# A two-block network on one core: a first turn split in two, column sums folded through DRAM, and residual rows behind three norms moved to GpSimd

## The chip, the core and the metric

The kernel runs on one core of one Trainium2 chip. The metric is the device time of one execution in microseconds. In what follows PE is TensorE, ACT is ScalarE, DVE is VectorE, POOL is GpSimd, and SP is the queue that starts most of the DMAs.

## The reference, cut to what matters

Two blocks of two layers each run one behind the other on 512 tokens of width 1024. Every layer takes scales, shifts and gates from a projection of a condition vector `c`, and uses them around a mixer (mLSTM, differential attention, RWKV-7, forgetting attention) and a feed-forward part.

```python
cs = jax.nn.silu(c)
for i in range(DEPTH):
    ada = cs @ w_ada[i] + b_ada[i]                       # 6 x 1024 values
    sh1, sc1, g1, sh2, sc2, g2 = jnp.split(ada, 6, axis=-1)
    u = x * (1.0 + sc1) + sh1
    y = mixer(u, ...)                                    # u @ w_in first
    x = _layer_norm(DEEPNORM_ALPHA * x + (1.0 + g1) * y, ln_g[i, 0], ln_b[i, 0])
    u = x * (1.0 + sc2) + sh2
    y = _conv_ffn(u, f_w_up[i], ...)                     # conv, gelu(g) * a, w_down
    x = _layer_norm(DEEPNORM_ALPHA * x + (1.0 + g2) * y, ln_g[i, 1], ln_b[i, 1])
...
mod = c_act @ mod_w[i] + mod_b[i]                        # the second block, the same way
```

## The kernel before, in words

Every product with a weight matrix is a `Linear`, and its work goes in **turns**. A turn gives a group of four PSUM banks; the two groups take turns. A weight tile is 1 MB (128 x 2048 floats; 768 KB in the down projections) and lies in a ring of three slots. SP loads it, ACT rounds it into `w_high` (`act_split`), DVE subtracts that into `w_low` (`dve_split`), and each product is three matmuls (`product`: high by high, high by low, low by high). A turn of a kind "f" linear has two tiles and 96 matmuls of 128 x 512; tiles are split two ahead of their use (`AHEAD`).

The input `u` of a linear comes out of `pe_turn` (transposes of `x_natural`), `act_turn` (scale and shift into `stage`, and the high part for odd k tiles) and `dve_turn` (the low part, and the high part for even k tiles): eight k tiles, 128 x 512 each.

**The projections of `c`.** They are cut into blocks of 512 columns, 4 at the start (`first_ada`, 0 to 3) and 48 spread over the turns of the linears from `m_qk` to `r_out` (`ada_ring`). For each of the 48, DVE multiplies eight 128 x 512 pieces by a column of silu(c) and sums them in `ada_acc` (`dve_ada`, eight instructions at the head of a turn). At the end of the same turn PE sums over the 128 partitions by four matmuls of a 128 x 128 part of `ada_acc` with a column of ones (`pe_ada`), and DVE adds the bias (`dve_ada_take`). The start must have blocks 0 and 2 before the k tiles 0 to 3 of the first `u`, and 1 and 3 before the k tiles 4 to 7.

**The start** is in `pe_first`, `dve_first` and `act_first`, and the order of the loads in `sync_program`: constants, blocks 0 and 2, weight tile 0, blocks 1 and 3, weight tile 1, seventeen small parameter rows, then the turns of `m_qk`.

**Rows behind a norm.** Behind three of the norms, `x_natural` is first used as the unit-variance rows, and its gain and shift are put on later by DVE, two 128 x 1024 instructions a token tile, at the head of the first four turns of `f0_up0`, `d_qk` and `f1_up0` (`dve_ln_rows`). In an `f*_up` turn DVE also runs the convolution of four banks (`f_a`, `f_g`), two `w_low` and the product of the halves.

**Gates** are stored to DRAM as columns (`act_gate_store`) and loaded back as rows on all partitions (`act_gate_load`); the residual on DVE (`dve_residual`) waits for them before it does anything else.

All engines run their programs in the order in which they are written; semaphores tie them together. POOL has nothing to do before the RWKV mixer.

## Time and profile before

| | us |
|---|---|
| median of three runs | 3160.3 |
| lowest, highest | 3153.82, 3168.22 |
| the profiled execution, its own time | 3167.36 |
| its span (first to last instruction) | 3166.0 |
| PE busy | 3006.9 |
| DVE, ACT, POOL busy | 1982.2, 1091.1, 97.6 |
| granted PE clock, mean | 0.982 |

The table is read so: PE is busy for 95% of the span, and the span is 1.4 us under the execution's own time. A saving on PE's own work or in its waits is a saving in the end; a saving on another engine is one only where PE waits for it. In a row of the trace the first number is the start in us, the second the time in us. A product of fp32 that is not split shows as two records. A count behind "x" merges records that follow each other.

### The profile page before, as it was taken

How to read it: one execution, taken by the hardware profiler on the slowest of the kernel's cores; microseconds unless marked ns; L12 is line 12 of the kernel's file. 1: busy time of each engine (PE TensorE's matmuls, PEld its weight loads, DVE VectorE, ACT ScalarE, POOL GpSimd, SP SyncE). 2: the span in 40 equal slices, each digit the busy share in tenths (PEclk: the TensorE clock that was granted, in tenths of full speed). 3: DMA queues.
4: the chain of work that ended last, by engine and by line, in shares of the span. 5: the costliest groups of instructions: out<-in, count | busy, mean ns of one | idle time of the engine just before them, and what ended most of it. 6: DMA issues, size and time to landing. Idle time of an engine off the chain costs nothing.

```text
span 3166.0 us, 46111 instructions
## 1 busy us (share of the span) xinstructions
PE 3006.9 (95%) x19763; PEld 2441.4 (77%) x19788; DVE 1982.2 (63%) x3051; ACT 1091.1 (34%) x1667; POOL 97.6 (3%) x116
## 2 busy tenths in 40 slices
PE   6999999999988999998999999999999998899999
PEld 5877788887866888884877778778887777778887
DVE  5856897787468896787455677654444255554353
ACT  2334432233146432233333333342224344542122
POOL 0000000000000000000002222000000001000000
PEclk8999999999999999998999999999999999999999
DMA  7751554545530454542210000233322220032232
GB/s 230 192 160 54 181 179 163 183 160 173 189 105 21 157 196 146 200 163 65 95 49 11 13 13 10 103 89 104 93 93 95 83 91 27 8 107 93 94 106 80
DMA packets 236545, 346.09 MB, mean 109 GB/s; under 512 B 19621, under 2 KB 121965, under 8 KB 236341
## 3 DMA queue, kind: packets, MB, share of 16 engines
q1 hardware_dynamic: 221236, 329.63, 32.3%
q10 hardware_dynamic: 15104, 13.52, 1.4%
q8 instruction: 155, 2.54, 0.3%
q14 instruction: 50, 0.40, 0.0%
HBM read 340.97 MB, written 2.15 MB: 108 GB/s over the span
## 4 chain that ended last, share of the span: by engine, by line
PE 80%; DVE 11%; ACT 4%; DMA 3%; issue 1%; SPq 0%; DVEq 0%; ACTq 0%
PE bank L141 79%; DVE w_tiles L150 2%; PE bank L144 1%; DVE w_low L150 1%; DMA first_ada<-in_w_ada 1%; ACT w_high L147 1%; DMA weight_ring<-in_d_w_in 1%; DVE ada_acc L162 1%; DVE w_g L150 1%; ACT w_tiles L147 1%; DVE x_natural L162 1%; ACT stage L147 1%; ACT L147 0%; DVE x_sm L168 0%; DVE x_natural L150 0%
## 5 line engine op out<-in xcount | busy, mean ns | idle before, releaser
L150 DVE TENSOR_TENSOR w_low<-weight_ring,w_high 128x2048 fp32r<-128x2048 f32 (+2 forms) x212 | 463.7, 2187 | 455.0 <-ACT w_high L147 454.8
L147 ACT ACTIVATE w_high<-weight_ring 128x2048 fp32r<-128x2048 f32 (+2 forms) x212 | 388.1, 1831 | 610.4 <-DMA weight_ring<-in_mlp_down 179.2
L141 PE MATMUL bank<-u_high,w_high 128*128 128x512 f32 x1472 | 577.3, 392 | 12.0 <-DVE w_low L150 6.2
L141 PE MATMUL bank<-u_high,w_low 128*128 128x512 f32 x1472 | 573.8, 390 | 0.0
L141 PE MATMUL bank<-u_low,w_high 128*128 128x512 f32 x1472 | 573.8, 390 | 0.0
L141 PE MATMUL bank<-w_high,u_high 128*128 128x512 f32 x896 | 353.1, 394 | 7.2 <-DVE w_low L150 2.5
L141 PE MATMUL bank<-w_low,u_high 128*128 128x512 f32 x896 | 350.9, 392 | 0.0
L141 PE MATMUL bank<-w_high,u_low 128*128 128x512 f32 x896 | 350.6, 391 | 0.0
L141 PEld LDWEIGHTS bank<-u_high,w_high 128*128 128x128 f32 x1472 | 276.9, 188 | 70.3 <-ACT stage L147 7.0
L141 PEld LDWEIGHTS bank<-u_high,w_low 128*128 128x128 f32 x1472 | 276.9, 188 | 58.3
L141 PEld LDWEIGHTS bank<-u_low,w_high 128*128 128x128 f32 x1472 | 277.0, 188 | 56.7
L162 DVE SCALAR_TENSOR_TENSOR ada_acc<-ada_ring,silu_c,ada_acc 128x512 f32<-128x512 f32 x336 | 252.6, 752 | 15.6 <-DVE ada_acc L162 0.5
L141 PEld LDWEIGHTS bank<-w_high,u_high 128*128 128x128 f32 x896 | 169.4, 189 | 45.8 <-DVE w_low L150 2.9
L141 PE MATMUL bank<-w_high,g_hidden_low 128*128 128x512 f32 x512 | 199.2, 389 | 0.0
L141 PE MATMUL bank<-w_high,g_hidden_high 128*128 128x512 f32 x512 | 199.2, 389 | 0.0
L141 PE MATMUL bank<-w_low,g_hidden_high 128*128 128x512 f32 x512 | 199.2, 389 | 0.0
L141 PEld LDWEIGHTS bank<-w_high,u_low 128*128 128x128 f32 x896 | 169.5, 189 | 36.0
L141 PEld LDWEIGHTS bank<-w_low,u_high 128*128 128x128 f32 x896 | 169.6, 189 | 34.9
L150 DVE TENSOR_TENSOR g_relu<-g_relu 128x512 f32<-128x512 f32 x64 | 44.3, 692 | 153.8 <-ACT g_relu L147 153.8
L141 PE MATMUL bank<-w_high,f_hidden_high 128*128 128x512 f32 x352 | 138.0, 392 | 1.5 <-DVE w_low L150 1.5
L141 PE MATMUL bank<-w_high,f_hidden_low 128*128 128x512 f32 x352 | 137.1, 389 | 0.0
L141 PE MATMUL bank<-w_low,f_hidden_high 128*128 128x512 f32 x352 | 137.0, 389 | 0.0
(411 smaller groups left out, 4398.9 us busy)
## 6 DMA issues: line engine op xcount, KB each, us to landing
ada_ring<-in_mod_w SPq DMA_DIRECT2D x48, 1024.0 KB, 7.6
weight_ring<-in_f_w_up SPq DMA_DIRECT2D x44, 1024.0 KB, 5.1
ada_ring<-in_w_ada SPq DMA_DIRECT2D x40, 1024.0 KB, 7.3
weight_ring<-in_mlp_up SPq DMA_DIRECT2D x32, 1024.0 KB, 5.5
weight_ring<-in_mlp_down SPq DMA_DIRECT2D x32, 1024.0 KB, 5.0
weight_ring<-in_f_w_down SPq DMA_DIRECT2D x24, 768.0 KB, 4.6
weight_ring<-in_m_w_in SPq DMA_DIRECT2D x16, 1024.0 KB, 10.4
weight_ring<-in_d_w_in SPq DMA_DIRECT2D x12, 1024.0 KB, 5.2
```

What stands on the lines that cost most here:

```text
L141: return self.e.matmul(out, l, r, start=start, stop=stop, skip_group_check=True)
L144: return self.e.transpose(out, in_, ident) if self.live else QUIET
L147: return self.e.activation(out, in_, f, **kw) if self.live else QUIET
L150: return self.e.tensor_tensor(out, a, b, op) if self.live else QUIET
L162: return self.e.scalar_tensor_tensor(out=out, in0=a, scalar=s, in1=b, op0=op0, op1=op1)
```

## The change

1. **The opening.** Weight tile 1 is loaded before blocks 1 and 3. The parameter rows come behind the loads of `m_qk`, and the small gate weights of ACT (`act_m_loads`) behind its whole opening. The splits of tiles 0 and 1 move ahead. The first turn of `m_qk` is done in two sets of k tiles: 0 to 3 for all four banks, then, once blocks 1 and 3 are there, 4 to 7. Block 1 is no longer summed by DVE: ACT scales its eight pieces and POOL adds them up by seven instructions.
2. **Column sums through DRAM.** `ada_acc` is stored to a DRAM scratch (SP, 256 KB), and loaded back so that the four 128-column parts lie side by side with partition and column regrouped. POOL adds four parts to one (128 x 256, then 128 x 128), and PE sums over groups of partitions by one matmul with a 128 x 4 pick matrix. The fold of a block is now due at the end of the turn behind the one in which it was summed. One block moves from `r_out` to `d_out`, and the 12 behind it by one turn. As their gate is ready later, gate `f0` is stored, awaited and loaded by ACT at the end of `f0_up0`.
3. **Residual rows.** The gain and shift behind the three norms go from DVE to POOL.

```diff
-                Linear("d_out", "t", a["d_w_out"][0], 2, wide(0), ada=blocks("m0", 11, 1))]
-        lin += [Linear("f1_up0", "f", up[1], 6, halves(0), ada=blocks("m1", 0, 6)),
+                Linear("d_out", "t", a["d_w_out"][0], 2, wide(0), ada=blocks("m0", 11, 1) + blocks("m1", 0, 1))]
+        lin += [Linear("f1_up0", "f", up[1], 6, halves(0), ada=blocks("m1", 1, 6)),
                 Linear("f1_dn0", "t", down[1], 2, wide(0), 12, 0, ada=blocks("kv", 0, 2)),
-                Linear("f1_up1", "f", up[1], 5, halves(6), ada=blocks("m1", 6, 5)),
...
             turn += x.turns
-            for i, b in enumerate(x.ada or ()):
-                self.ada_bank[b] = x.group(i)
+            for i, b in enumerate(x.ada):
+                if summed is not None:
+                    self.takes[x.name, i] = summed
+                summed = b
+        self.takes["r_r", 0] = summed
...
         self.sp_weight(sp, 0)
+        self.sp_weight(sp, 1)
         for b in (1, 3):
             self.sp_first(sp, b)
-        self.sp_weight(sp, 1)
+        self.sp_linear(sp, "m_qk")
         for name, dst, src, last in self.param_parts():
             if dst[0] > 0:
                 sp.dma_start(self.rows[dst[1]:dst[2], dst[0], :], src).then_inc(*self.params_in.landed(*(("rows",) if last else ())))
-        self.sp_linear(sp, "m_qk")
+        sp.wait_ge(self.G, "first summed", 1)
...
                 if w >= AHEAD:
                     self.sp_weight(sp, w)
+                if name != "d_out" or w > L.first + i * per:
+                    self.sp_sum_in(sp)
             if i < len(L.ada):
...
                 sp.wait_ge(self.V, "ada used", b - 1, s)
+                if s:
+                    self.sp_sum_out(sp, b - 1)
             src = w[s * 512:(s + 1) * 512, :].rearrange("(k p) n -> p k n", p=P)
             dst = self.aring[:, s, :].rearrange("p (k n) -> p k n", k=4)
             sp.dma_start(dst, src).then_inc(*self.ada_in[s].landed(b))
+
+    def sp_sum_out(self, sp, b):
+        sp.wait_ge(self.V, "ada summed", b)
+        if b - 2 >= len(self.ada_first):
+            sp.wait_ge(self.fold_in, b - 2)
+        sp.dma_start(self.fold_rows[b % 2], self.aacc[:]).then_inc(*self.fold_out.landed(b))
+        self.stored_sum = b
+
+    def sp_sum_in(self, sp):
+        b = self.stored_sum
+        if b > self.loaded_sum:
+            tile, passed = self.sum_place(b)
+            sp.wait_ge(self.fold_out, b)
+            if passed:
+                sp.wait_ge(*passed)
+            if b > len(self.ada_first):
+                sp.wait_ge(self.T, "ada", b - 1)
+            src = self.fold_rows[b % 2].rearrange("a n -> (a n)").rearrange("(q p m) -> p q m", q=4, p=P)
+            sp.dma_start(tile.rearrange("p (q m) -> p q m", q=4), src).then_inc(*self.fold_in.landed(b))
+            self.loaded_sum = b
+
+    def sum_place(self, b):
...
+    def pool_sums(self, g, *names, rows=None):
+        for name in names:
+            for i in range(self.lin[name].turns):
+                if rows and i < TT:
+                    self.pool_ln_rows(g, *rows[:3], i, rows[3])
+                if (name, i) in self.takes:
+                    b = self.takes[name, i]
+                    parts = self.sum_place(b)[0].rearrange("p (q m) -> p q m", q=4)
+                    g.wait_ge(self.fold_in, b)
+                    g.tensor_tensor(parts[:, 0:2, :], parts[:, 0:2, :], parts[:, 2:4, :], ALU.add).then_inc(*self.G.up())
+                    g.wait_ge(self.G)
+                    g.tensor_tensor(parts[:, 0, :], parts[:, 0, :], parts[:, 1, :], ALU.add).then_inc(*self.G.up("folded", b))
...
                 between()
 
-    def pe_ada(self, pe, b):
-        bank = self.ada_bank.get(b, 7)
-        pe.wait_ge(self.V, "ada summed", b)
-        if bank in self.free:
-            pe.wait_ge(*self.free[bank])
-        for j in range(4):
-            m = pe.matmul(self.bank[bank][:, j:j + 1], self.aacc[:, j * P:(j + 1) * P], self.ones[:, 0:1], True, True)
-        m.then_inc(*self.T.up("ada", b))
-        self.free[bank] = (self.V, "mod", b)
-
-    def dve_ada_take(self, v, b):
-        _, bias, at, _ = self.ada_blocks[b]
-        v.wait_ge(self.T, "ada", b)
-        v.tensor_tensor(self.mod[:, at:at + 4], self.bank[self.ada_bank.get(b, 7)][:, 0:4], bias, ALU.add).then_inc(
-            *self.V.up("mod", b))
+    def pe_ada(self, pe, name, i):
+        if (name, i) in self.takes:
+            b, bank = self.takes[name, i], self.lin[name].group(i)
+            pe.wait_ge(self.G, "folded", b)
...
-                    v.wait_ge(self.V)
                     if b > len(self.ada_first):
-                        v.wait_ge(self.T, "ada", b - 1)
+                        v.wait_ge(self.fold_out, b - 1)
                     v.tensor_scalar(self.aacc[:], src, col, None, ALU.mult).then_inc(*self.V.up())
...
-    def dve_ln_rows(self, v, st, tiles, n, t, turned):
+    def pool_ln_rows(self, g, st, tiles, n, t, turned):
         x = self.X[:, t, :]
-        v.wait_ge(self.T, "turned", turned, KT - 1)
-        v.wait_ge(self.ln_in[n], "rows")
-        v.wait_ge(self.V)
-        v.tensor_tensor(x, x, tiles[0][:], ALU.mult).then_inc(*self.V.up())
-        v.wait_ge(self.V)
-        v.tensor_tensor(x, x, tiles[1][:], ALU.add).then_inc(*self.V.up("rows", st, t))
+        g.wait_ge(self.T, "turned", turned, KT - 1)
+        g.wait_ge(self.ln_in[n], "rows")
+        g.tensor_tensor(x, x, tiles[0][:], ALU.mult).then_inc(*self.G.up())
+        g.wait_ge(self.G)
+        g.tensor_tensor(x, x, tiles[1][:], ALU.add).then_inc(*self.G.up("rows", st, t))
...
         scale, shift = self.plain_modulation(0)
         for h in range(2):
+            if h == 0:
+                self.act_split(a, 0)
             a.wait_ge(self.V, "first", h)
             a.wait_ge(self.V, "first", 2 + h)
-            if h:
-                self.act_split(a, 0)
             self.act_turn(a, "m u", scale, shift, range(4 * h, 4 * h + 4))
-        self.act_split(a, 1)
+            if h == 0:
+                self.act_split(a, 1)
+                for k in range(KT):
+                    src = self.first_w[:, 1, k, :]
+                    a.wait_ge(self.first_in[1][k // 4], "first")
+                    a.activation(src, src, ACT.Copy, scale=self.cs[:, k:k + 1]).then_inc(*self.A.up("first scaled", k))
...
-        self.pe_turn(pe, "m u", lambda t: self.X[:, t, :])
-        for b, bank in ((1, 3), (3, 2)):
+        x = lambda t: self.X[:, t, :]
+        self.pe_turn(pe, "m u", x, range(6))
+        self.pe_first_turn(pe, range(4))
+        for b, bank in ((1, 6), (3, 7)):
             pe.wait_ge(*self.free[bank])
             self.pe_first_summed(pe, b, bank)
             self.free[bank] = (self.V, "first", b)
+        self.pe_turn(pe, "m u", x, range(6, KT))
+        self.pe_first_turn(pe, range(4, KT))
+        self.pe_ada(pe, "m_qk", 0)
+
+    def pe_first_turn(self, pe, kts):
+        L = self.lin["m_qk"]
+        for s in range(2):
+            w = L.tile(0, s)
...
+            for kt in kts:
+                for n in range(2):
+                    b = 2 * s + n
+                    bank, o = L.group(0) + b, kt * 256 + n * P
+                    if kt == 0 and bank in self.free:
+                        pe.wait_ge(*self.free[bank])
+                    pe.wait_ge(self.V, "u", "m u", kt)
+                    m = self.product(pe, self.bank[bank][:], [y[:, w % SLOTS, o:o + P] for y in (self.whigh, self.wlow)],
+                                     [y[:, kt, :] for y in self.u], kt == 0, kt == KT - 1)
+                    if kt == KT - 1:
+                        m.then_inc(*self.T.up("sum", "m_qk", 0, b))
+                        self.free[bank] = (self.V, "got", "m_qk", 0, b)
+            if kts[-1] == KT - 1:
+                self.T.mark("used", w)
...
         self.dve_first_sums(v, 2)
         self.dve_first_take(v, 0, 6)
         self.dve_first_take(v, 2, 7)
+        self.dve_split(v, 0)
         self.dve_turn(v, "m u", range(4))
-        self.dve_first_sums(v, 1)
+        self.dve_split(v, 1)
         self.dve_first_sums(v, 3)
-        self.dve_first_take(v, 1, 3)
-        self.dve_first_take(v, 3, 2)
-        self.dve_split(v, 0)
+        self.dve_first_take(v, 1, 6)
+        self.dve_first_take(v, 3, 7)
         self.dve_turn(v, "m u", range(4, KT))
-        self.dve_split(v, 1)
+        v.wait_ge(self.core_in, "core")
+        v.tensor_reduce(self.pick, self.ident.rearrange("p (r g) -> p g r", g=4), ALU.add).then_inc(*self.V.up("pick"))
...
+    def pool_first_sums(self, g, b):
+        acc = self.first_acc[:, b - 1, :]
+        for k in range(1, KT):
+            g.wait_ge(self.A, "first scaled", k)
+            g.wait_ge(self.G)
+            g.tensor_tensor(acc, acc if k > 1 else self.first_w[:, b, 0, :], self.first_w[:, b, k, :], ALU.add).then_inc(*self.G.up())
...
         f, st = self.f[l], f"f{l}"
-        self.act_gate_load(a, st, f["gb"][:])
+        if l:
+            self.act_gate_load(a, st, f["gb"][:])
         self.act_norm_rows(a, f["ln"], 2 * l + 1)
         self.act_turn(a, st, self.fold[:, 0:8], self.fold[:, 8:16])
         self.act_ffn_up(a, l, st + "_up0", 0, None)
-        for gate in (("x",) if l else ("d",)):
-            self.act_gate_store(a, gate)
+        if l:
+            self.act_gate_store(a, "x")
+        else:
+            self.act_gate_store(a, "f0")
+            self.act_gate_load(a, "f0", f["gb"][:])
+            self.act_gate_store(a, "d")
...
     def pool_diff(self, g):
+        self.pool_sums(g, "m_out")
+        self.pool_sums(g, "f0_up0", rows=("m", self.m_ln, 0, "f0"))
+        self.pool_sums(g, "f0_dn0", "f0_up1", "f0_dn1")
+        self.pool_sums(g, "d_qk", rows=("f0", self.f[0]["ln"], 1, "d u"))
+        self.pool_sums(g, "d_v")
...
     def pool_rwkv(self, g):
+        self.pool_sums(g, "d_out")
+        self.pool_sums(g, "f1_up0", rows=("d", self.d_ln, 2, "f1"))
+        self.pool_sums(g, "f1_dn0", "f1_up1", "f1_dn1", "r_r")
```

**Where instructions move.** At the start of DVE's program, the names are `first_acc` for the sums of blocks 1 to 3, `u_high` and `u_low` for the input. Before:

```order
L165 CAST u_high<-stage 128x512
L150 TENSOR_TENSOR u_low<-stage,u_high 128x512 x2
L156 TENSOR_SCALAR first_acc<-first_ada,silu_c 128x512
L162 SCALAR_TENSOR_TENSOR first_acc<-first_ada,silu_c,first_acc 128x512 x7
L156 TENSOR_SCALAR first_acc<-first_ada,silu_c 128x512
L162 SCALAR_TENSOR_TENSOR first_acc<-first_ada,silu_c,first_acc 128x512 x7
L150 TENSOR_TENSOR modulation_columns<-bank,param_columns 128x4 x2
L150 TENSOR_TENSOR w_low<-weight_ring,w_high 128x2048
L165 CAST u_high<-stage 128x512
```

The same place of DVE's program now:

```order
L150 TENSOR_TENSOR modulation_columns<-bank,param_columns 128x4 x2
L150 TENSOR_TENSOR w_low<-weight_ring,w_high 128x2048
L165 CAST u_high<-stage 128x512
L150 TENSOR_TENSOR u_low<-stage,u_high 128x512 x2
L165 CAST u_high<-stage 128x512
L150 TENSOR_TENSOR u_low<-stage,u_high 128x512 x2
L150 TENSOR_TENSOR w_low<-weight_ring,w_high 128x2048
L156 TENSOR_SCALAR first_acc<-first_ada,silu_c 128x512
L162 SCALAR_TENSOR_TENSOR first_acc<-first_ada,silu_c,first_acc 128x512 x7
L150 TENSOR_TENSOR modulation_columns<-bank,param_columns 128x4 x2
```

Both `w_low` stand ahead of the late sums, and one of the two late sums is gone.

POOL's program around the start of `f0_up0`, where before it had nothing (`ada_sum_top` is the place of a loaded sum, `m_ln_g` and `m_ln_b` are gain and shift):

```order
L150 TENSOR_TENSOR ada_sum_top<-ada_sum_top 128x256
L150 TENSOR_TENSOR ada_sum_top<-ada_sum_top 128x128
L150 TENSOR_TENSOR x_natural<-x_natural,m_ln_g 128x1024
L150 TENSOR_TENSOR x_natural<-x_natural,m_ln_b 128x1024
L150 TENSOR_TENSOR ada_sum_top<-ada_sum_top 128x256
L150 TENSOR_TENSOR ada_sum_top<-ada_sum_top 128x128
L150 TENSOR_TENSOR x_natural<-x_natural,m_ln_g 128x1024
L150 TENSOR_TENSOR x_natural<-x_natural,m_ln_b 128x1024
```

The rows of a token tile stand between two folds and wait for nothing but the transposes and the fold ahead of them, so the second pair can follow the first at once.

SP's queue in a turn of `m_qk`, before:

```order
L186 DMA weight_ring<-in_m_w_in 128x8x256 x2
L186 DMA ada_ring<-in_w_ada 128x4x512 x2
```

and now:

```order
L186 DMA weight_ring<-in_m_w_in 128x8x256
L186 DMA m_o<-fold_rows 128x4x128
L186 DMA weight_ring<-in_m_w_in 128x8x256
L186 DMA ada_ring<-in_w_ada 128x4x512
L186 DMA fold_rows<-ada_acc 128x512
L186 DMA ada_ring<-in_w_ada 128x4x512
```

The load of the last sum stands between the two weight tiles, the store of the next between the two halves of a block.

## Rows read from the trace of the kernel before

**Rows 1.** The page, part 4: shares of the chain that ended last.

```profile
PE 80%; DVE 11%; ACT 4%; DMA 3%; issue 1%; SPq 0%; DVEq 0%; ACTq 0%
```

**Rows 2.** The chain in order of time, opening: start us, us, what.

```profile
10.30 27.16 DMA first_ada<-in_w_ada
...
51.73 1.92 ACT w_high L147
...
56.02 92.46 PE bank L141 x408
```

**Rows 3.** Timeline of the opening: DVE and PE on the late blocks.

```profile
38.01 5.54 DVE L162 SCALAR_TENSOR_TENSOR first_acc<-first_ada,silu_c,first_acc 128x512 f32<-128x512 f32 x7
...
49.58 1.87 PE L141 MATMUL bank<-ones,first_acc 128*128 128x1 f32 x8 [4.04 <-DVE first_acc L162]
```

**Rows 4.** Tile weight_ring, 0 to 90 us: issue to landing of five weight tiles.

```profile
DMA to landing us min/median/max: 10.2/11.7/29.0
```

**Rows 5.** Stretches: us, busy (x) of PE, PEld, DVE, ACT, POOL, clock, DMA, GB/s.

```profile
36.90:60.80 23.90, 8.49 (x27) 7.36 (x28) 17.46 (x25) 7.52 (x8) 0.00 (x0) 0.50 0.78 245
...
228.10:234.90 6.80, 6.33 (x19) 5.36 (x20) 2.69 (x3) 0.13 (x1) 0.00 (x0) 0.50 1.03 372
```

**Rows 6.** Timeline of PE in m_qk: two folds, and six steps between matmuls.

```profile
80.17 0.95 PE L141 MATMUL bank<-ones,ada_acc 128*128 128x1 f32 x8
...
101.29 0.39 PE L141 MATMUL bank<-u_high,w_low 128*128 128x512 f32 x1
...
102.65 0.39 PE L141 MATMUL bank<-u_high,w_low 128*128 128x512 f32 x1
102.88 0.94 PE L141 MATMUL bank<-ones,ada_acc 128*128 128x1 f32 x8
```

**Rows 7.** Timeline of PE: folds at the ends of m_v, m_o and d_v turns.

```profile
202.93 0.95 PE L141 MATMUL bank<-ones,ada_acc 128*128 128x1 f32 x8
...
228.57 1.87 PE L141 MATMUL bank<-ones,ada_acc 128*128 128x1 f32 x8 [2.77 <-DVE ada_acc L162]
...
254.32 0.95 PE L141 MATMUL bank<-ones,ada_acc 128*128 128x1 f32 x8
...
878.96 1.05 PE L141 MATMUL bank<-ones,ada_acc 128*128 128x1 f32 x8 [4.13 <-DVE ada_acc L162]
```

**Rows 8.** Timeline of DVE in f0_up0: from one pair of rows to the next.

```profile
376.51 0.43 DVE L165 CAST u_high<-stage 128x512 fp32r<-128x512 f32 x1
...
383.40 1.23 DVE L150 TENSOR_TENSOR x_natural<-x_natural,m_ln_g 128x1024 f32<-128x1024 f32 x1
...
386.00 0.49 DVE L156 TENSOR_SCALAR ada_acc<-ada_ring,silu_c 128x512 f32<-128x512 f32 x1
...
406.69 1.22 DVE L150 TENSOR_TENSOR x_natural<-x_natural,m_ln_g 128x1024 f32<-128x1024 f32 x1
```

**Rows 9.** Timeline before the forgetting attention: DVE and POOL beside each other.

```profile
2594.44 0.69 DVE L150 TENSOR_TENSOR x_qn<-x_q,x_sm 128x512 f32<-128x512 f32 x1
2594.48 1.55 POOL L150 TENSOR_TENSOR x_kn<-x_k,x_sm 128x512 f32<-128x512 f32 x1 [587.75 <-DVE x_sm L177]
2595.17 1.42 DVE L150 TENSOR_TENSOR x_qn<-x_qn,x_gain 128x512 f32<-128x512 f32 x1
...
2596.11 1.63 POOL L150 TENSOR_TENSOR x_kn<-x_kn,x_gain 128x512 f32<-128x512 f32 x1
```

**Rows 10.** POOL's groups by form: busy us, mean ns, idle before.

```profile
L150 POOL TENSOR_TENSOR w_tiles<-w_g,w_const 128x256 f32<-128x256 f32 x40 | 29.0, 726 | 1737.0 <-DVE w_tiles L150 1678.1 <-PE bank L141 58.9
...
L150 POOL TENSOR_TENSOR w_tiles_b<-w_tiles_b,w_lnp 128x512 f32<-128x512 f32 x7 | 8.9, 1277 | 38.5 <-DMA w_lnp<-in_rw_lnb 38.5
```

**Rows 11.** Tile gate_rows, 505 to 530 us: issue to landing of gate d's store.

```profile
L186 ACTq DMA_DIRECT2D gate_rows<-modulation_columns x1: 384/384/384, 514.7 to 514.7; - x1
...
DMA to landing us min/median/max: 13.2/13.2/13.2
```

**Rows 12.** DMA issues, 365 to 380 us: KB each, us to landing.

```profile
f_gate_rows<-gate_rows ACTq DMA_DIRECT2D x1, 512.0 KB, 3.8
```

More of the change, by code:

```diff
@@ L491, in linears @@
         at = turn = 0
-        self.ada_bank = {}
+        self.takes, summed = {}, None
         for x in lin:
@@ new lines, in sum_place @@
+    def sum_place(self, b):
+        name, i = next(k for k, x in self.takes.items() if x == b)
+        last = lambda name: (self.T, "used", self.lin[name].tile(self.lin[name].turns - 1, len(self.lin[name].pieces) - 1))
+        if name in ("m_qk", "m_v") or (name, i) == ("m_o", 0):
+            return self.m_o[:, 3, 512:D], (self.V, "first summed", 3)
+        if name in ("d_qk", "d_v"):
+            return self.d_o[:, 3, 512:D], last("f0_dn1")
+        if name == "r_r":
+            return self.r_k[:, 3, 512:D], last("f1_dn1")
+        return self.sum_top[:], (self.T, "gate sums", "m") if name[0] == "m" else (self.T, "used", self.lin["d_out"].tile(0, 0)) if name == "d_out" else None
@@ L704, in pe_keep, with pe_linear_f @@
             pe.matmul(self.bank[bank][:], x[:, 0:P], x, True, True)
-    def pe_linear_f(self, pe, name, u, ends):
+    def pe_linear_f(self, pe, name, u, ends, first=0):
         L = self.lin[name]
-        for i in range(L.turns):
+        for i in range(first, L.turns):
             for s in range(2):
@@ L1308, in pool_m @@
     def pool_m(self, g):
+        self.pool_first_sums(g, 1)
+        self.pool_sums(g, "m_qk", "m_v", "m_o")
         self.join(g, self.G, "m cell start")
```

75 lines of the change are left out of this document (44 added, 31 removed).

## The prediction

> **What bounds the kernel now.** I read the shares of the chain first: 80% of it is PE [rows 1]. So time is won by taking work off PE or by ending a wait of PE. Then I read the chain in order of time for the opening: PE's first long run starts only at 56.02 us, behind a load, the sums on DVE and a split [rows 2, 3]. Then PE's own timeline turn by turn: the distance of two folds is one turn. It is 102.88 - 80.17 = 22.71 us; six steps between matmuls are 1.36 us, one is 0.2267, so 96 matmuls are 21.76 and the fold costs 0.95 [rows 6]. Last, DVE's timeline in `f0_up0`: from one pair of rows to the next it needs 406.69 - 383.40 = 23.29 us, more than PE's 22.71 [rows 8]. There DVE is the engine that decides, and anything that slows DVE slows the kernel.
>
> **The change part by part.** The sum is made against the span, 3166.0 us; the profiled execution took 1.4 us more, and the median of the runs, 3160.3, is 7.1 under that execution. The sum's difference is put on the median.
>
> *Folds on PE.* Four fp32 products, eight records, become one, two records. A quarter of 0.95 is 0.24; the step from the last long matmul into and out of the fold may stay whole, which makes it 0.40. I take 0.35: 0.60 saved, 48 times, **-28.8** (0.55 to 0.71: -26 to -34).
>
> *Two waits for a sum.* PE waited 2.77 us in `m_o` and 4.13 in `d_v` for `ada_acc` [rows 7]. The new fold takes the sum of the turn before, which has long been there. In `m_o` the turns around the first wait are 228.57 - 202.93 = 25.64 and 254.32 - 228.57 = 25.75 instead of 22.71, 6.0 us together; half clock for 6.8 us stands behind the wait [rows 5, 7]. I price `d_v` the same. The weight tile that is due next was split before the sum in both. **-12.0** (-7 to -12).
>
> *The opening.* Weight tile 0 lands at 4.2 + 29.0 = 33.2 us [rows 4]. ACT's split takes 1.9, DVE's the 2.3 between it and the first matmul, one k tile 1.1: the first matmul stands at 38.6 instead of 56.02 [rows 2, 8], and the first 48 matmuls end by 52. But the second set waits for blocks 1 and 3, which land behind one more MB, 3.3 us later (2.7 to 5.6). DVE adds block 3 by eight instructions, 6.2 us with the first [rows 3]; POOL adds block 1 by seven of 1.27 us [rows 10], 8.9. If they run side by side the later ends at 52.6; if one at a time, from 44.4 to 58.7. Then two folds of 1.9 [rows 3], a take, ACT and DVE on k tile 4: PE resumes at 63. The clock is at 0.50 by then, as in the long lull of before [rows 5]: 4.8 us at half speed for 11 matmuls, 8.4 for 37 more, 76.2. DVE must still make the k tiles (until 66), sum its next block (6.1), do six convolution steps (4.7) and split tile 2 (2.3): 79.6 is the start of the second turn, against 80.97. **-1.4** one at a time, -5.6 side by side; +4 if the tiles land late. The parameter rows are due at about 150 and leave SP at about 115: nothing.
>
> *Rows and folds on POOL.* POOL's 128 x 256 takes 0.73, its 128 x 512 takes 1.27 [rows 10], so 0.54 more for 256 elements: 2.35 for 1024, 4.7 a pair, and 0.73 + 0.46 for a fold. What do they cost DVE? Here the trace has a plain case: at 2595.17 DVE's instruction took 1.42 where its like took 0.69, POOL's took 1.55 and 1.63 instead of 1.1 and 1.3, and each ends where the other's work begins [rows 9]. They took the time one after the other. The Trainium skill (SBUF — State Buffer, "SBUF: two separate sides" and "Who interferes with whom") says why: GpSimd holds the port pair it shares with VectorE for a whole instruction, and a VectorE instruction with two SBUF inputs, or a copy in a 2-port mode, waits for it. The trace agrees at this place, and by that rule the gain of this part turns into a loss; were there no such lock, the part would be free.
>
> On DVE the casts, the low parts, the sums of `ada_acc`, both `w_low` and the product of the halves have both inputs in SBUF or are copies; only the convolution reads PSUM.
>
> (a) First turns of `f0_up0`, `d_qk`, `f1_up0`. The rows may start when the transposes are done, which is when DVE makes the k tiles. Pair 0, a fold and pair 1 follow at once: 4 x 2.35 + 1.2 = 10.6 us of POOL against 7.4 us of DVE (four casts of 0.43, eight low parts of 0.69). The last k tile is ready at 18.0 instead of 7.6; PE ends the turn at 18.0 + 1.4 + 10.9 + 0.35 = 30.7 instead of 23.3 by its own work. **+22.5** for three (0 to +32).
>
> (b) Turns two and three of `f0_up0` and `f1_up0`. Without the rows DVE needs 23.29 - 2.60 = 20.69 [rows 8]; POOL's 5.9 falls on it for 0.7 to all: 24.8 to 26.6 against PE's 22.11. Twice 2.7 to 4.5, less a slack of 1.1 (DVE splits the first turn's next tile at 18.0 + 6.1 + 3.2 + 2.3 = 29.6, PE wants it at 30.7): 4.3 to 7.9, I take 6.1. **+12.2** for two linears (0 to +16). In all other turns a fold's 1.2 us lies within DVE's slack (20.7 + 1.2 against 22.1). `d_qk` has no convolution on DVE and takes its rows without loss.
>
> (c) What DVE lost before goes: four turns of 0.58 less the slack of 1.1, twice, **-2.4**.
>
> *Gate f0.* ACT now stores, waits and loads at the end of `f0_up0`. The store of gate d at this very place took 13.2 us to land, beside the weight tiles [rows 11]; a gate load took 3.8 [rows 12]. DVE waits for the gate in front of its splits: 514.7 + 13.2 + 3.8 + 1.9 = 533.6. `f0_dn0` begins at about 512.9 (the sixth turn of 22.7 us behind a start at 375.8 ends at 512.9 with the losses above), its tiles are 36 matmuls, 8.2 us, and the third is due at 529.3. 4.3 us and 1.7 for the clock behind it, **+6** (0 to +9; with the 3.8 us of the load for the store too, nothing).
>
> *Small.* `d_out` gets a second block of sums, 6.2 us on DVE where a later residual is awaited: **+1** (0 to +3). Half clock in the new gaps of the first turns: the wait in `m_o` of 2.77 us brought it [rows 5, 7], these gaps are at most 2.3 us: **+3** (0 to +10). The way through DRAM is due 16 us after its load is issued; the longest landing of the rows that bears on it is 13.2 [rows 11]: nothing, while it holds.
>
> Sum: -28.8 - 12.0 - 1.4 + 22.5 + 12.2 - 2.4 + 6 + 1 + 3 = **+0.1**. Span 3166.1, median 3160.4.
>
> **The rivals.**
> A, the forecast: PE's gain of about 42 us is given back by DVE and POOL on one port. 3160, and 3145 to 3176 by the bounds of its terms.
>
> B, POOL costs DVE little. The instructions seen in rows 9 are few; with longer ones the chip may let DVE through more often, or pair 1 comes late. Then (a), (b) and the clock go and the opening is side by side: -28.8 - 12.0 - 5.6 - 2.4 + 6 + 1 = -41.8, **3118.5**. Against it: rows 9, where nothing ran side by side.
>
> C, slower: the port holds DVE for all of POOL's time, and the gaps bring half clock. The place is the first turn of the three linears. With the upper ends of (a) and (b), 32 and 16, 10 for three stretches of 6.8 us at half speed, 9 for the gate, 2 for `d_out` and no gain in the opening: -28.8 - 12.0 - 2.4 + 32 + 16 + 10 + 9 + 2 = +25.8, **3186**. It decides when a gap in the making of k tiles passes the 2.8 us of the one in `m_o`: two POOL instructions between two of DVE would do it.
>
> D, the folds don't do what they say: the store and the load stand in SP's queue behind 1 MB tiles, and PE waits for `folded` at the ends of turns. At 3 us in twelve turns, +36 beside A, 3196.
>
> **How the numbers follow.** Within 0.5% (3144.5 to 3176.1) is about what a measurement of this kernel can tell from no change. Chances: A 0.52, of which 0.03 fall under 3144.5 and 0.06 over 3176; B 0.28; C 0.15, a fifth of it within 0.5%; D 0.05. Faster 0.31, same 0.46, slower 0.23. The range takes in B and most of C: 3114 to 3182. The likeliest case's own range is 3145 to 3176.
>
> **What would show it.** In the profile after: folds of two records, and turns of 22.1 us in `m_qk`; no wait at the ends of `m_o` and `d_v`; first long matmul near 39, start of the second turn near 79.6. The first turn of `f0_up0` lasts 30 us, with DVE casts and low parts of up to 3 us beside POOL instructions of 2.35 to 3; under B they keep 0.43 and 0.69. At the start of `f0_dn0` a wait of PE for `w_low` of some 4 us. The prediction is wrong if PE's turns in `f0_up0` are 22.1 from the first on (B), or if PE waits for POOL at the ends of turns (D).

## The result, and the profile of the changed kernel

The changed kernel took 3185.6 us (median of 4 runs, 3181.6 to 3190.9), the kernel before 3157.1 (4 runs, 3153.1 to 3168.2): 1.0083 of its time, 95% interval 1.0064 to 1.0102. It is slower by 0.8%. The forecast was 3160.4, no change, with a range from 3114 to 3182.

The two profiled executions lie closer together than the medians, 3180.2 us of span against 3166.0. That of before was a long one of its kind, that of the change the shortest of four. So both kernels were traced once more (below), and the second pair, 3176.2 against 3151.2, is 25.0 apart.

The page of the changed kernel, first busy times, then the shares of the chain that ended last:

```profile
span 3180.2 us, 45838 instructions
...
PE 2991.7 (94%) x19475; PEld 2417.2 (76%) x19500; DVE 2019.1 (63%) x3020; ACT 1097.0 (34%) x1675; POOL 252.3 (8%) x243
...
PE 52%; DVE 7%; ACT 3%; DMA 1%; issue 1%; DVEq 0%; ACTq 0%
```

The 52% can't be set against the 80% of before [rows 1]. The chain of the changed kernel could be followed back only to 1153 us, so its shares add up to 64% of the span and not to 99%.

The stretches below are cut at the folds, the short products at the ends of turns, which both kernels have at the same places of the program. Microseconds, from the PE timelines of two traces of each kernel:

| stretch | before | before, 2nd | after | after, 2nd |
|---|---|---|---|---|
| start to the last fold of `m_o` | 254.3 | 249.7 | 243.5 | 242.9 |
| to the first of `m_out` (mLSTM cell) | 90.0 | 90.0 | 95.4 | 95.5 |
| to the first of `f0_up0` | 53.3 | 54.4 | 62.9 | 62.6 |
| turns two to six of `f0_up0` | 114.5 | 114.4 | 117.1 | 117.3 |
| `f0_dn0` | 67.2 | 67.2 | 74.7 | 73.0 |
| `f0_up1`, `f0_dn1` | 169.9 | 169.9 | 164.9 | 164.9 |
| to the first of `d_qk` | 34.6 | 34.4 | 41.8 | 41.8 |
| rest of `d_qk`, `d_v` | 119.5 | 114.4 | 110.0 | 110.0 |
| to the first of `d_out` (heads) | 137.1 | 134.5 | 138.2 | 139.3 |
| to the first of `f1_up0` | 53.1 | 52.3 | 65.5 | 65.9 |
| turns two to six of `f1_up0` | 114.8 | 114.8 | 116.9 | 117.0 |
| `f1_dn0`, `f1_up1`, `f1_dn1` | 238.8 | 238.3 | 233.0 | 232.3 |
| the rest | 1718.8 | 1716.9 | 1716.3 | 1713.5 |

Where nothing else happens, the change wins: the seven turns of `f0_up1` and `f0_dn1` are 4.9 us shorter together. PE's timeline in `m_qk` shows why (start us, us, what; before: [rows 6]):

```profile
99.96 0.28 PE L141 MATMUL bank<-small,m_o 128*128 128x4 f32 x2
...
121.97 0.28 PE L141 MATMUL bank<-small,m_o 128*128 128x4 f32 x2
```

A turn is 22.01 us and was 22.71: a fold costs 0.25 and saves 0.70.

**First turns.** DVE and then POOL at the start of `f0_up0`; a bracket is the idle time before an instruction and what ended it:

```profile
372.84 2.59 DVE L150 TENSOR_TENSOR u_low<-stage,u_high 128x512 fp32r<-128x512 f32 x1 [0.18 <-ACT u_high L147]
375.36 2.60 DVE L165 CAST u_high<-stage 128x512 fp32r<-128x512 f32 x1
378.00 1.95 DVE L150 TENSOR_TENSOR u_low<-stage,u_high 128x512 fp32r<-128x512 f32 x2
380.00 2.50 DVE L165 CAST u_high<-stage 128x512 fp32r<-128x512 f32 x1
382.54 3.31 DVE L150 TENSOR_TENSOR u_low<-stage,u_high 128x512 fp32r<-128x512 f32 x2
```

```profile
372.24 2.65 POOL L150 TENSOR_TENSOR x_natural<-x_natural,m_ln_g 128x1024 f32<-128x1024 f32 x1 [24.51 <-PE bank L144]
374.97 2.71 POOL L150 TENSOR_TENSOR x_natural<-x_natural,m_ln_b 128x1024 f32<-128x1024 f32 x1
377.65 1.76 POOL L150 TENSOR_TENSOR ada_sum_top<-ada_sum_top 128x256 f32<-128x256 f32 x2
379.37 2.84 POOL L150 TENSOR_TENSOR x_natural<-x_natural,m_ln_g 128x1024 f32<-128x1024 f32 x1
382.29 2.40 POOL L150 TENSOR_TENSOR x_natural<-x_natural,m_ln_b 128x1024 f32<-128x1024 f32 x1
```

The first turns of `f1_up0` and `f0_up0` as stretches (columns as in [rows 5]):

```profile
1081.00:1114.00 33.00, 28.09 (x102) 21.57 (x100) 28.25 (x27) 11.76 (x16) 12.21 (x6) 0.81 0.33 120
372.80:401.80 29.00, 24.50 (x97) 19.16 (x98) 27.15 (x25) 10.47 (x14) 11.66 (x6) 0.93 0.33 118
```

A cast that takes 0.43 us [rows 8] takes 2.60, and ends 0.3 us behind the end of POOL's instruction (377.96 against 377.68): beside one long instruction of POOL, DVE gets one of its own done. The first turn lasts 29.0 us (372.81 to the fold at 401.80) and was 21.9.

**Gate f0.** PE, then ACT's queue, then DVE at the start of `f0_dn0`:

```profile
541.42 0.79 PE L141 MATMUL bank<-w_high,f_hidden_high 128*128 128x512 f32 x1 [5.75 <-DVE w_low L150]
...
560.74 0.28 PE L141 MATMUL bank<-small,ada_sum_top 128*128 128x4 f32 x2
```

```profile
521.53 0.38 ACTq L186 DMA_DIRECT2D gate_rows<-modulation_columns  x1
...
532.27 0.33 ACTq L186 DMA_DIRECT2D f_gate_rows<-gate_rows  x1
```

```profile
539.60 1.76 DVE L150 TENSOR_TENSOR w_low<-weight_ring,w_high 128x1536 fp32r<-128x1536 f32 x1 [12.79 <-DMA f_gate_rows<-gate_rows]
```

The store is out at 521.5, the load can start at 532.3 and lands 7.3 later; DVE's split stands behind it.

**The joins.** All engines meet before the mLSTM cell and before the attention heads. DVE at the first and, below the dots, at the second, then PE at both:

```profile
239.11 0.49 DVE L156 TENSOR_SCALAR ada_acc<-ada_ring,silu_c 128x512 f32<-128x512 f32 x1
239.64 5.54 DVE L162 SCALAR_TENSOR_TENSOR ada_acc<-ada_ring,silu_c,ada_acc 128x512 f32<-128x512 f32 x7
245.09 2.28 DVE L150 TENSOR_TENSOR w_low<-weight_ring,w_high 128x2048 fp32r<-128x2048 f32 x1
247.30 0.15 DVE L150 TENSOR_TENSOR modulation_columns<-bank,param_columns 128x4 f32<-128x4 f32 x1
...
908.03 5.62 DVE L162 SCALAR_TENSOR_TENSOR ada_acc<-ada_ring,silu_c,ada_acc 128x512 f32<-128x512 f32 x7
913.57 2.29 DVE L150 TENSOR_TENSOR w_low<-weight_ring,w_high 128x2048 fp32r<-128x2048 f32 x1
...
916.82 0.43 DVE L165 COPY d_kh<-d_qk 128x512 f32<-128x512 f32 x1
```

```profile
243.51 0.28 PE L141 MATMUL bank<-small,ada_sum_top 128*128 128x4 f32 x2
247.55 0.98 PE L144 MATMUL bank<-core_constants,m_gates 4*128 4x4 f32 x8 [3.76 <-DVE modulation_columns L150]
...
917.27 3.73 PE L141 MATMUL bank<-core_constants 128*128 128x512 bf16 x11 [6.64 <-DVE d_kh L165]
```

The same two places of PE's program in the kernel before:

```profile
255.57 0.63 PE L144 MATMUL bank<-core_constants,m_gates 4*128 4x4 f32 x8 [0.30 <-DVE modulation_columns L150]
...
906.37 3.96 PE L141 MATMUL bank<-core_constants 128*128 128x512 bf16 x11 [2.06 <-DVE small L156]
```

The waits were 0.30 and 2.06 and are 3.76 and 6.64. PE no longer waits for the sum at the end of `m_o` and `d_v`. It comes to the join earlier, and there it waits until DVE has made that same sum. The mean granted clock is 0.976 and 0.977 in the two traces of the change, 0.982 and 0.986 in those of before. Behind the first of these waits the granted clock is 0.50, the level of 1.2 GHz, for 13.6 us (columns as in [rows 5]):

```profile
247.30:260.90 13.60, 13.01 (x27) 5.66 (x29) 1.98 (x10) 7.02 (x14) 0.00 (x0) 0.50 0.50 174
```

### The profile page after: what moved, and what is told of

It reads as the page before. It is cut to its first block, busy times and chain, and to the rows that moved or that the text cites. A ratio compares the mean times of both kernels' runs of the same rounds, so it can differ in the third digit from the quotient of the medians.

```text
span 3180.2 us, 45838 instructions
## 1 busy us (share of the span) xinstructions
PE 2991.7 (94%) x19475; PEld 2417.2 (76%) x19500; DVE 2019.1 (63%) x3020; ACT 1097.0 (34%) x1675; POOL 252.3 (8%) x243
## 4 chain that ended last, share of the span: by engine, by line
PE 52%; DVE 7%; ACT 3%; DMA 1%; issue 1%; DVEq 0%; ACTq 0%
PE bank L141 51%; DVE w_tiles L150 2%; PE bank L144 1%; DVE w_g L150 1%; ACT w_tiles L147 1%; DVE x_natural L162 1%; DMA weight_ring<-in_f_w_down 0%; DVE x_sm L168 0%; DVE w_low L150 0%; DVE x_q L162 0%; ACT L147 0%; ACT stage L147 0%; ACT w_high L147 0%; DVE w_tiles_b L150 0%; ACT x_p L147 0%
## 5 line engine op out<-in xcount | busy, mean ns | idle before, releaser
L141 PE MATMUL bank<-u_high,w_high 128*128 128x512 f32 x1472 | 584.5, 397 | 37.9 <-DVE u_low L150 20.3
L141 PEld LDWEIGHTS bank<-u_high,w_low 128*128 128x128 f32 x1472 | 280.0, 190 | 59.5
L162 DVE SCALAR_TENSOR_TENSOR ada_acc<-ada_ring,silu_c,ada_acc 128x512 f32<-128x512 f32 x336 | 261.9, 780 | 15.2
L141 PEld LDWEIGHTS bank<-w_high,u_high 128*128 128x128 f32 x896 | 169.0, 189 | 46.1 <-DVE w_low L150 3.2
L141 PE MATMUL bank<-w_low,f_hidden_high 128*128 128x512 f32 x352 | 138.2, 393 | 0.0
## 6 DMA issues: line engine op xcount, KB each, us to landing
weight_ring<-in_m_w_in SPq DMA_DIRECT2D x16, 1024.0 KB, 10.6
```

What stands on the lines that cost most here:

```text
L141: return self.e.matmul(out, l, r, start=start, stop=stop, skip_group_check=True)
L162: return self.e.scalar_tensor_tensor(out=out, in0=a, scalar=s, in1=b, op0=op0, op1=op1)
```

## Experiments

Each kernel is measured beside the kernel before on the same chip, whose medians were 3156.9, 3155.7 and 3156.2 us in the three groups. "Less than the changed kernel" is a difference of medians of different groups. The ratios to the kernel before give less for two of them: against 1.0083 of the changed kernel, 1.0058 for the early gate is about 8 us and 1.0069 for the early sum about 4, and both intervals overlap that of the changed kernel. So these two sizes are uncertain by several us, and what the edits did is read from the stages of the traces.

### The rows back on DVE

```
-        self.pool_sums(g, "f0_up0", rows=("m", self.m_ln, 0, "f0"))
+        self.pool_sums(g, "f0_up0")
...
+        self.dve_ffn_up(v, l, st + "_up0", 0, lambda t: self.dve_ln_rows(v, before, tiles, 2 * l, t, st))
```

The same for `f1_up0` and `d_qk`.

> The changed kernel with the twelve pairs of residual rows back on DVE, as before; the folds stay on POOL. Port theory (POOL's rows stop DVE's copies and two-input instructions): the first turns of the three linears lose 7.2, 7.1 and 9.8 us in the changed kernel, turns two and three of the two up-projections 14 together, so 38 us go; the rows on DVE cost 1.29 a turn over PE's 22.0 in four turns less 1.1, twice, +8. So 3185.6 - 30 = 3156, first turn of f0_up0 near 22, DVE's casts beside the transposes 0.43. Rival (the fold's store and load in SP's queue make the weight tiles late): nothing changes there, 3186, and the first turn stays at 29.

Measured 3160.8 us, 1.0011 of before (0.9998 to 1.0025): 24.8 less than the changed kernel. DVE makes its casts in 0.43 again, and the first fold of `f0_up0` is at 397.46. So SP's queue, unchanged here, isn't what made the first turns long. The 5 us that are missing from the 30 can't be given to one place. In this trace the first turns of `f0_up0` and `d_qk` are 23.7 and 23.9 us and not 22, the five turns behind the first of both up-projections lose 10.9 in all and not 8, and the first turn of `f0_dn0`, behind gate f0, is 46.1 against 41.8; but the traced execution, 3164.4, is the longest of the ten.

### The rows on POOL in the kernel before

```
+    def pool_diff(self, g):
+        self.pool_ln_rows(g, "m", self.m_ln, 0, "f0")
+        self.pool_ln_rows(g, "f0", self.f[0]["ln"], 1, "d u")
```

POOL works on pairs 0 and 1 at the transposes; pairs 2 and 3 wait for DVE's last split of the first and second turn.

> The kernel before with the twelve pairs of rows on POOL alone; pairs 0 and 1 at the transposes, 2 and 3 behind the last split of turns 0 and 1; no other part of the change. Port theory: three first turns lose 7 to 10 us each, two later pairs in each up-projection 2 to 4 each, what DVE lost before (2.4) comes back: +24 + 12 - 2.4 = +33, 3190. Rival (POOL costs DVE nothing): 3157 - 2.4 = 3155.

Measured 3188.8 us, 1.0100 (1.0066 to 1.0133). The part alone costs 32 us, in a kernel that has nothing else of the change. Both runs together show from both sides what the rows on POOL cost, 25 to 32 us. My terms (a), (b) and (c) had 32.3 for it.

### POOL's rows in pieces of 256

```
-        g.tensor_tensor(x, x, tiles[0][:], ALU.mult)
+        for q in range(4):
+            c = slice(256 * q, 256 * q + 256)
+            g.tensor_tensor(x[:, c], x[:, c], tiles[0][:, c], ALU.mult)
...
```

The addition of the shift is cut in four in the same way.

> The changed kernel with each of POOL's row instructions of 1024 elements cut into four of 256. Theory lock per instruction, total unchanged (POOL holds DVE for about as long as it works, in pieces): POOL's pair takes 8 x 0.73 = 5.8 instead of 5.3 us, DVE's copies take one piece each, the first turn of f0_up0 stays at 28 to 31 and the time at 3186, 3180 to 3192. Rival (only a long instruction keeps DVE out, between short ones it gets in at no cost): the first turns lose half, -12 to -20, 3170.

Measured 3164.3 us, 1.0025 (1.0013 to 1.0037): the rival, and 6 us past its 3170, though DVE does not get in at no cost. DVE and POOL in the first turn of `f0_up0`:

```profile
372.81 0.95 DVE L165 CAST u_high<-stage 128x512 fp32r<-128x512 f32 x1
373.80 2.25 DVE L150 TENSOR_TENSOR u_low<-stage,u_high 128x512 fp32r<-128x512 f32 x2
375.97 0.96 DVE L165 CAST u_high<-stage 128x512 fp32r<-128x512 f32 x1
...
383.02 8.00 DVE L162 SCALAR_TENSOR_TENSOR ada_acc<-ada_ring,silu_c,ada_acc 128x512 f32<-128x512 f32 x7
```

```profile
371.33 4.17 POOL L150 TENSOR_TENSOR x_natural<-x_natural,m_ln_g 128x256 f32<-128x256 f32 x4 [24.52 <-PE bank L144]
375.58 4.23 POOL L150 TENSOR_TENSOR x_natural<-x_natural,m_ln_b 128x256 f32<-128x256 f32 x4
```

The cast takes 0.95 instead of 2.60 though POOL is busy for longer in all, 8.4 us a pair instead of 5.4. What DVE loses isn't POOL's time; it is one POOL instruction for each of its own. My prediction had added the two engines' times; that is right only where the instructions of both are about equally long, as in [rows 9].

### POOL's rows beside the convolution

```
+                if rows and i < TT and name != "d_qk":
+                    g.wait_ge(self.A, "acc", name, i, 0)
```

> The changed kernel with POOL's pair in each of turns 0 to 3 of f0_up0 and f1_up0 held until ACT has made the turn's first f_a, so that it runs beside DVE's convolution, which reads PSUM. Theory (POOL stops only copies and instructions with two SBUF inputs): 3.2 of the 5.3 us lie beside four convolution steps of 0.79, which keep that length; the rest holds a split: 2.2 a turn less DVE's slack of 1.3, +7 in all, against -17 and -14 that go: 3162. Rival (POOL stops every DVE instruction): the steps beside it take 1.5 to 3 us, 4 us a turn in eight turns, +32: 3187.

Measured 3184.4 us, 1.0095 (1.0071 to 1.0119), the rival's time, but not for its reason. ACT makes the first `f_a` while DVE still adds its columns, so in the first turn of `f0_up0` the rows came beside the column sum: seven steps took 10.2 us instead of 5.5. In the second turns they came beside a low part of the hidden half and the start of the sum. Only in the first turn of `f1_up0` did they come where I wanted them (DVE, then POOL):

```profile
1094.15 3.17 DVE L162 SCALAR_TENSOR_TENSOR f_a<-bank,param_columns,f_a 128x511 f32<-128x511 f32 x4
1097.24 3.71 DVE L150 TENSOR_TENSOR w_low<-weight_ring,w_high 128x2048 fp32r<-128x2048 f32 x1
```

```profile
1093.75 2.57 POOL L150 TENSOR_TENSOR x_natural<-x_natural,d_ln_g 128x1024 f32<-128x1024 f32 x1 [38.43 <-ACT f_a L147]
1096.40 2.40 POOL L150 TENSOR_TENSOR x_natural<-x_natural,d_ln_b 128x1024 f32<-128x1024 f32 x1
```

Four steps that read PSUM take 3.17 us, as alone; the split behind them, with both inputs in SBUF, takes 3.71 instead of 2.28. The Trainium skill (SBUF — State Buffer, "Who interferes with whom") says that a VectorE instruction contends when it has two SBUF inputs or is a copy in a 2-port mode; these rows agree. My price for this kernel, 3162, was wrong because the wait that I chose did not bring the rows to the convolution.

### POOL's rows at the start of f0_dn0 and f1_dn0

```
+    def pool_rows_late(self, g, st, tiles, n, turned):
+        g.wait_ge(self.V, "hidden", turned + "_up0", 11)
+        for t in range(TT):
+            self.pool_ln_rows(g, st, tiles, n, t, turned)
```

> The changed kernel with POOL's eight pairs of f0_up0 and f1_up0 moved to the start of f0_dn0 and f1_dn0, behind the last hidden half; d_qk's stay. Theory (it is not the work on POOL but its place that costs: in f0_dn0 DVE has 14 us of slack a turn, and waits for the gate in its first 12): -17 and -14 go, +2 to +8 in f1_dn0, where DVE's splits stand beside it: 3157 to 3163. Rival (20 us of POOL make the residuals late, PE waits for banks and splits at turn 1): 10 us each, 3175.

Measured 3170.7 us, 1.0047 (1.0032 to 1.0062), between the two; the traced execution, 3157.7, is the shortest of the eight. All turns of `f0_up0` and `f1_up0` are 22.0 now. In `f1_dn0` the cost is back, and it is the port and not late residuals (DVE, then PE):

```profile
1215.30 17.81 DVE L162 SCALAR_TENSOR_TENSOR ada_acc<-ada_ring,silu_c,ada_acc 128x512 f32<-128x512 f32 x7
1233.03 3.67 DVE L150 TENSOR_TENSOR w_low<-weight_ring,w_high 128x1536 fp32r<-128x1536 f32 x2
```

```profile
1235.09 0.79 PE L141 MATMUL bank<-w_high,f_hidden_high 128*128 128x512 f32 x1 [9.37 <-DVE w_low L150]
```

Seven steps of 0.79 became six of 2.7 to 2.8 and one of 1.1. DVE has some 14 us of slack in such a turn (33 us less four splits of 1.75, a sum of 6 and four residuals of 1.4), and this ate 12 of it in front of a split that PE wanted.

### Gate f0 earlier

```
+        if l == 0:
+            self.act_gate_store(a, "f0")
         self.act_turn(a, st, self.fold[:, 0:8], self.fold[:, 8:16])
...
+            if name == "f0_up0" and i == 1:
+                self.act_gate_load(a, "f0", f["gb"][:])
```

> The changed kernel with the store of gate f0 ahead of the transposes of f0_up0 and its load behind the first turn. Gate theory: DVE no longer waits 12.8 us for the rows, PE's wait of 5.75 and the half clock behind it go, the turn of 41.8 becomes 32.9: -8.9, 3176.7. Rival (the third weight tile of f0_dn0 lands late anyway, behind the gate's packets): PE still waits for w_low, at most -3, 3183.

Measured 3170.5 us, 1.0058 (1.0034 to 1.0083): 15 less than the changed kernel. The first turn of `f0_dn0` is 32.89 in its trace, PE's own. In the traces of the seven kernels and repeats that keep the late gate this turn takes 40.0 to 48.4 us, and the load of the gate's rows lands in 6.3 to 13.5 us; the 41.8 of the first trace, with 7.3, is at the low end. In the two traces of the changed kernel the turn is 8.9 and 7.3 us longer than here; the 15 of the medians holds more than that, or other executions waited longer, and no trace says which.

### The sum ahead of the splits at the joins

```
+            early = i == L.turns - 1 and name in ("m_o", "d_v")
+            if early:
+                self.dve_ada(v, L.ada[i])
+                self.dve_ahead(v, name, i, 0)
...
```

> The changed kernel with DVE's column sum ahead of the splits, in place of behind the first, in the last turn of m_o and of d_v. Theory (what ended last at both joins is DVE's sum, which PE now overtakes): the waits of 3.76 at the cell and 6.64 at the heads shrink by 3 and 5.4 and the half clock behind the first by 2: -10, 3175. Rival (the weight tiles of the next linear or the column take are what is late): at most -3, 3183.

Measured 3174.2 us, 1.0069 (1.0048 to 1.0091): 11.5 less. PE at both joins of this kernel:

```profile
244.64 0.63 PE L144 MATMUL bank<-core_constants,m_gates 4*128 4x4 f32 x8 [0.66 <-ACT m_o L147]
...
905.20 2.54 PE L141 MATMUL bank<-core_constants 128*128 128x512 bf16 x11 [2.88 <-DVE small L156]
```

The waits are 0.66 and 2.88 instead of 3.76 and 6.64. The stretch with the cell is 89.2 us instead of 95.4, below the 90.0 of before; that with the heads is 133.2 instead of 138.2. Together the two stretches give back 11.2 us.

### Both kernels once more

> The kernel before once more, for a second trace. Luck theory (the profiled execution from which the sum was made, 3167.4 against a median of 3156, was long by stretches of half clock in stages that the change does not touch, 27.3 us of it between the splits of r_v and r_out, where others show 13.7): this trace is shorter by 5 to 10 us there, and the stages up to the end of f1_dn1 agree within 2 us. Rival (the waits in m_o and d_v are what varies): these turns differ by over 2 us.

3152.6 us, span 3151.2. Two things were luck in the first trace. The stretch between the splits of `r_v` and `r_out`, which nobody touched, is shorter by 4.4 us here. These are the stretches of before, first and second trace (columns as in [rows 5], the clock being the seventh figure):

```profile
1581.30:2023.40 442.10, 408.45 (x7671) 337.10 (x7688) 285.40 (x562) 156.65 (x301) 77.59 (x96) 0.97 0.10 31
```

```profile
1569.40:2007.10 437.70, 404.07 (x7675) 335.15 (x7692) 284.96 (x562) 156.74 (x301) 77.60 (x96) 0.98 0.11 31
```

And the wait in `d_v` is 0.58 instead of 4.13 [rows 7], in the second trace:

```profile
871.58 1.05 PE L141 MATMUL bank<-ones,ada_acc 128*128 128x1 f32 x8 [0.58 <-DVE ada_acc L162]
```

The wait in `m_o`, 2.77, is in both. So the rival has a part too: the stages that the change touches did vary, by 4.6 us up to the last fold of `m_o`, of which 3.3 are the start of the second turn, by 5 in the stretch with `d_v` and by 3 in the heads. My forecast for this trace, that the stages up to `f1_dn1` agree within 2 us, was wrong.

> The changed kernel once more, for a second trace. If the store of gate f0 is what varies, the turn of f0_dn0 that took 41.8 us takes 40 to 48 here, as in the kernels that kept it (46.1, 44.4, 48.4, 40.6), and the landing of its store 15 to 22 us; the first turns of the three linears repeat within 1 us. Rival (all terms vary alike): the first turns differ by over 2 us.

3177.5 us, span 3176.2. The first turn of `f0_dn0` took 40.2, at the low end of what I had expected. The store of gate f0 landed in 10.8 us and not in 15 to 22: of the two DMAs behind that turn it is the load that varies. The stretches with first turns repeat within 0.5 us of the first trace.

### Three repairs together

```
-        self.dve_residual(v, st + "_dn0", st, f["gb"], ALPHA)
+        self.dve_residual(v, st + "_dn0", st, f["gb"], ALPHA, rows=lambda t: self.dve_ln_rows(v, before, tiles, 2 * l, t, st))
```

with the pairs between the column sum and the splits of the first turn; the pairs of `d_qk` on DVE where they were before; and the two edits above, the early gate and the sum first.

> Three repairs together: the pairs of rows on DVE, those of f0_up0 and f1_up0 in the slack of the first turn of f0_dn0 and f1_dn0, d_qk's where they were; gate f0 stored and loaded early; the sum ahead of the splits at both joins. From the run with the rows on DVE, 3160.8: the rows' loss in four turns goes (-8), the gate -9 to -15, the joins -10: 3130. Rival (the three share one slack, DVE in f0_dn0 is now late with splits): -12 in all, 3149.

Measured **3126.4 us** (3121.8 to 3131.7), 0.9910 of before (0.9896 to 0.9925): faster than both kernels. DVE in the first turn of `f0_dn0`:

```profile
510.18 5.54 DVE L162 SCALAR_TENSOR_TENSOR ada_acc<-ada_ring,silu_c,ada_acc 128x512 f32<-128x512 f32 x7
515.83 1.23 DVE L150 TENSOR_TENSOR x_natural<-x_natural,m_ln_g 128x1024 f32<-128x1024 f32 x1
...
528.54 1.23 DVE L150 TENSOR_TENSOR x_natural<-x_natural,m_ln_b 128x1024 f32<-128x1024 f32 x1
529.87 0.69 DVE L150 TENSOR_TENSOR stage<-bank,f_gate_rows 128x512 f32<-128x512 f32 x1
```

The rows end just before the first residual, and the turn is 32.89 us long. All turns of `f0_up0` behind the first are 22.0.

### The opening without POOL

```
+        self.dve_first_sums(v, 1)
         self.dve_first_sums(v, 3)
```

in the kernel with the three repairs, and ACT's scaling and POOL's additions left out.

> The kernel with the three repairs, and block 1 of the opening summed by DVE, ahead of block 3, without ACT's scaling and POOL's additions. Port theory (POOL and DVE slowed each other: seven additions took 10.7 instead of 8.9 us, DVE's seven steps 9.0 instead of 5.5): DVE adds block 1 from 43.9 to 50 while block 3 is still landing, and block 3 until 56.1; the second fold starts at 56.2 instead of 57.3: -1, 3125.4. Rival (POOL's help is worth its six us): +5, 3131.

Measured 3131.7 us, 0.9910 (0.9874 to 0.9945), not to be told from 3126.4. It is also the number of the rival, but not for its reason: this trace is 12.5 us longer than that of the three repairs, and 13.4 stand behind the last fold of `f1_dn1`. In the opening it is shorter: the fold of block 3 starts at 55.36 instead of 56.45, and the second turn at 76.17 instead of 77.26. So no gain from POOL's help is seen there: DVE's seven steps take 5.54 alone, and 9.02 when POOL works beside the first four of them.

## Why the prediction was wrong, point by point

The sum of my terms was +0.1; the medians are 28.6 apart, the second traces 25.0. Three small sums in it were off: four casts and eight low parts are 7.2 us and not 7.4, DVE's work before the second turn adds up to 79.1 and not 79.6, and 8.9 and 6.2 one behind the other from 44.4 end at 59.5 and not 58.7. All three are under 1 us.

*Folds.* Right in kind, too small: 0.70 each and not 0.60, -34 instead of -28.8. All of the 0.95 but 0.25 goes.

*Two waits for a sum: the step that failed.* I wrote **-12.0**, "the weight tile that is due next was split before the sum in both". That looked at the next tile only. What stands right behind both places is a join, and there every engine's queue must be empty: the sum that PE no longer awaited in the turn it awaited 4 us later, together with a split and a take behind it. In the cell the stretch grew by 5.6 us, in the heads by 4.8 (second traces), though each has a fold that is 0.7 shorter: 11.8 that no term of mine held. The kernel with the sum first gives back 11.5. The waits themselves were also less than I took: the 4.13 in `d_v` is 0.58 in the second trace, so what went in the turns is about 5.5, not 12. In place of -12.0 stands about +6 (-5.5 + 11.8), and these 18 us alone are more than half of the miss.

*The opening.* -1.4 forecast; the second turn starts 2.9 us earlier in the first traces and 0.3 in the second. The first long matmul is at 34.99, not 38.6. DVE's sum could start only at 47.51, when block 3 had landed, and POOL's first three additions, 1.29 to 1.36 each, were made or begun by then. Where the two met they took turns, but not at the sum of their times: POOL's additions took up to 1.52 and DVE's first four steps 1.56 to 1.66, one pair each 1.67 us, where 1.27 and 0.75 are 2.02. DVE's last three steps, alone again, took 0.75.

*(a) First turns.* +22.5 and 3 for the clock. By the turns' own ends it is 7.1 in `f0_up0` (29.0 against 21.9), about 8 around `d_qk` and 9.8 in `f1_up0` (31.6 against 21.9): 25. This was the main mechanism, and it holds. The number hides a premise that did not: I had taken PE's gaps in these turns as at most 2.3 us, and they reach 3.15 in `f0_up0` and 3.13 in `f1_up0`. `f1_up0` costs more, 28.1 us of PE's time at a mean clock of 0.81 in that turn against 24.5 at 0.93 in `f0_up0`'s. The way in which I came to it was wrong in one point: DVE doesn't lose POOL's busy time but one POOL instruction for each of its own, as the pieces of 256 show.

*(b) and (c).* +12.2 - 2.4 = +9.8; the five turns behind the first grew by 6.2 and 5.6 us beside the folds' gain: 11.8.

*Gate f0.* +6, bounded by 9. 8.9 and 7.3 in the two traces, 15 by the medians of the run that undoes it. The store was near my row (the load went out 10.6 to 11.5 us behind it; 13.2 in [rows 11]); the load took 6.3 to 13.5 and not the 3.8 of [rows 12], which was read where one weight tile was in flight for its first us only; in the trace of the change two were. That row should have been an end of the range and not the value.

*The base.* I read waits and clock from one execution that was 10 us above the usual one, and put the difference on the median. That counted the `d_v` wait as a gain that the median run doesn't have to give.

*Small.* The +1 for `d_out` and the +3 for the clock can't be told apart. From the end of the last long product in front of a first turn to the turn's own first one PE takes 11.9 us in the changed kernel at `f0_up0` and 11.8 at `f1_up0`, where it took 8.8 and 8.5 in the kernel before (second traces: 11.6 and 12.3, against 9.9 and 7.8). With the rows back on DVE it is 11.6 at both, so this isn't the rows. A part is seen: PE waits 0.86 us in front of k tile 1 for DVE's take of the fold, in both traces of the change and in neither of before. In the first traces the mean clock of these stretches is 0.74 and 0.62 in the changed kernel and 1.00 and 0.81 in the kernel before. Why it fell, and so the rest of these 2 to 4.5 us at each place, stays open: no run was made on it.

*The rivals.* C came nearest by its time, 3186, and by both of its halves in kind: POOL held DVE, and half clock stood for 41 us in and in front of the three first turns, 10 us in the first trace of before. That its time fits is luck all the same. It held -12 for the two waits, 32 and 16 for (a) and (b) where 25 and 11.8 were measured, and the joins, 11.8, were in no rival. D is out: the one wait of PE for POOL is that for block 1 of the opening, 4.68, and with the rows on DVE the same queue of SP goes with 3160.8. B's price was wrong as well as its reason: even with the three losses repaired the gain is 29 us, not 42.

## What to carry to other kernels

When a wait of the bounding engine goes, follow that engine to the next join and ask which engine comes last there; work that a wait had hidden must be moved ahead of what it delays, as was done here, or behind the join, which no run tried. POOL, which shares a port with DVE, takes over work here at the price of one of its instructions for each one of DVE's beside it: keep its instructions short, put them beside work that reads PSUM (seen here in one turn only, with no gain in time), or leave the work where it was and use a turn with slack. Take a second trace before a sum rests on a single wait.
